# One encoder layer in float32 on one core: attention scores as full-array matmuls, shifted tiles, and VectorE work reordered around the router

## What is computed

```python
x = layer_norm(x, emb_ln_g, emb_ln_b)
z = x @ w_in + b_in
q, k, v, u_sg, v_sg, glu_a, glu_g = jnp.split(z, SPLIT_POINTS, axis=-1)
a = neighbourhood_attention(q, k, v, rpb) @ w_a_o      # 8 heads of 64, 4x16 queries see 4x32 keys
bb = (gelu(u_sg) * spatial(w_s, layer_norm(gelu(v_sg)))) @ w_b_o
c = silu(layer_norm(depthwise_conv(glu_a * sigmoid(glu_g)))) @ w_c_o
g = sigmoid(x @ w_gate + b_gate)                       # three gates of width 1024
m = (g0 * a + g1 * bb + g2 * c) @ w_o + b_o
x = layer_norm(ALPHA * x + m, ln1_g, ln1_b)
f = grouped_moe(x, w_router, b_router, w_e1, w_e3, w_e2)  # 16 experts, two for each token
x = layer_norm(ALPHA * x + f, ln2_g, ln2_b)
```

## Time and profile before

| what | value |
| --- | --- |
| median of 3 runs | 785.61 us (785.34 to 785.99) |
| the profiled execution: time, and span of its instructions | 787.25 us, 785.5 us |
| TensorE busy | 756.5 us (96%) |
| VectorE, ScalarE, GpSimd busy | 610.3, 428.2, 71.0 us |
| mean granted clock of TensorE | 0.988 of full speed |
| DMA | 175.53 MB, mean 223 GB/s |

### The profile page before, as it was taken

The page is one execution under the profiler, slowest core; times in us unless marked ns, Lnnn a source line. Parts: engine busy times, 40 slices in busy tenths (PEclk is TensorE's granted clock), DMA queues, the critical chain, the costliest instruction groups (busy, mean ns, idle before and its releaser), DMA issues.

```text
span 785.5 us, 10752 instructions
## 1 busy us (share of the span) xinstructions
PE 756.5 (96%) x3580; PEld 619.8 (79%) x3580; DVE 610.3 (78%) x827; ACT 428.2 (55%) x577; POOL 71.0 (9%) x94
## 2 busy tenths in 40 slices
PE   3999999999999999999999979999999999999995
PEld 3888878888888888888888857888888888888873
DVE  5699977675777875634547888999999999999977
ACT  5422134547432234623231365888888888888861
POOL 5000000000000000000011112111111111110314
PEclk9999999999999999999999988999999999999998
DMA  9844557132444343323279677999999999999882
GB/s 299 243 108 100 175 150 207 55 92 72 117 123 131 111 138 104 103 86 108 81 244 350 213 258 237 335 387 382 382 381 380 387 387 368 375 368 369 255 171 111
DMA packets 137490, 175.53 MB, mean 223 GB/s; under 512 B 15419, under 2 KB 75559, under 8 KB 137431
## 3 DMA queue, kind: packets, MB, share of 16 engines
q1 hardware_dynamic: 128896, 154.95, 58.7%
q0 software_dynamic: 7616, 19.34, 8.2%
q10 hardware_dynamic: 934, 0.69, 0.3%
HBM read 164.06 MB, written 19.11 MB: 233 GB/s over the span
## 4 chain that ended last, share of the span: by engine, by line
PE 92%; DVE 4%; ACT 2%; DMA 1%; issue 1%; POOL 0%; SPq 0%; DVEq 0%; ACTq 0%
PE bank L1834 27%; PE bank L1836 27%; PE bank L1835 27%; PE bank L2129 2%; PE bank L1870 1%; PE bank L2050 1%; DMA x_in<-in_x_sample_dram 1%; PE bank L1829 1%; PE bank L2144 1%; PE bank L2230 1%; PE bank L1880 1%; DVE w_lo L1053 1%; PE bank L2089 1%; PE bank L2220 0%; PE bank L2221 0%
## 5 line engine op out<-in xcount | busy, mean ns | idle before, releaser
L1053 DVE TENSOR_TENSOR w_lo<-raw,w_hi 128x1024 fp32r<-128x1024 f32 x103 | 125.1, 1221 | 80.4 <-ACT w_hi L721 80.1
L721 ACT CAST w_hi<-raw 128x1024 fp32r<-128x1024 f32 x103 | 107.1, 1048 | 105.3 <-PE bank L1836 100.7
L1834 PE MATMUL bank<-xT_hi,w_hi 128*128 128x512 f32 x352 | 139.9, 397 | 2.9 <-DVE xT_lo L1091 1.8
L1836 PE MATMUL bank<-xT_hi,w_lo 128*128 128x512 f32 x352 | 138.8, 394 | 0.0
L1835 PE MATMUL bank<-xT_lo,w_hi 128*128 128x512 f32 x352 | 137.8, 392 | 0.0
L1834 PEld LDWEIGHTS bank<-xT_hi,w_hi 128*128 128x128 f32 x352 | 66.5, 189 | 18.2 <-issue 3.4
L1834 PE MATMUL bank<-w_hi,xgT_hi 128*128 128x512 f32 x198 | 80.1, 404 | 0.8 <-issue 0.8
L1836 PEld LDWEIGHTS bank<-xT_hi,w_lo 128*128 128x128 f32 x352 | 66.4, 189 | 14.7
L1835 PEld LDWEIGHTS bank<-xT_lo,w_hi 128*128 128x128 f32 x352 | 66.6, 189 | 14.5
L1836 PE MATMUL bank<-w_hi,xgT_lo 128*128 128x512 f32 x198 | 77.5, 392 | 0.0
L1835 PE MATMUL bank<-w_lo,xgT_hi 128*128 128x512 f32 x198 | 77.3, 390 | 0.0
(11 more groups left out here) (288 smaller groups left out, 1532.6 us busy)
## 6 DMA issues: line engine op xcount, KB each, us to landing
raw_more<-in_w_e_dram SPq DMA_DIRECT2D x48, 512.0 KB
raw<-in_w_e_dram SPq DMA_DIRECT2D x48, 512.0 KB, 9.3
raw_late<-in_w_e_dram SPq DMA_DIRECT2D x48, 512.0 KB
raw_rows<-in_w_e_dram SPq DMA_DIRECT2D x48, 512.0 KB, 9.6
raw<-in_w_in_dram SPq DMA_DIRECT2D x28, 512.0 KB, 6.5
raw<-in_w_gate_dram SPq DMA_DIRECT2D x24, 512.0 KB, 3.8
y_scratch<-zeros SPq DMA_DIRECT2D x8, 512.0 KB, 5.0
raw<-in_w_o_dram SPq DMA_DIRECT2D x8, 512.0 KB, 3.7
```

The costliest lines, as they stand in the source:

```text
L721: act.copy(hi_slot(j), raw_slot(j)).then_inc(hi_cast, 1)
L1053: dve.tensor_tensor(lo_slot(j), raw_slot(j), hi_slot(j).bitcast(F32), ALU.subtract).then_inc(lo_cast, 1)
L1834: pe.matmul(out, hi_l, hi_r, start=start, stop=False)
L1836: return pe.matmul(out, lo_l, hi_r, start=False, stop=stop)
```

## The change

1. **Scores.** `q_pair` replaces `qT`. It holds, for two head pairs in turn, both sequences and four windows, a 128x128 block: head 0's queries on partitions 0 to 63 in columns 0 to 63, head 1's on partitions 64 to 127 in columns 64 to 127, and zeros elsewhere. One matmul over all 128 partitions then gives both heads' scores of a window: 4 for a group in place of 8. ScalarE writes the blocks with four instructions of 64 partitions in place of two of 128, and waits for the scores that read the buffer before. GpSimd writes the zeros once, after unit 2 and after the normalised input, which shares the memory, is stored.
2. **Where tiles lie.** Four 16-byte tiles become one of 64 bytes, `moments`, so everything behind them lies 64 bytes lower. `mT_hi` gets `LINE` and stays where it was. In the built program `xT_hi`, `xT_lo` and the first two branches now start on a multiple of 128 bytes; `q_pair`, `kT`, `v_win`, `vs`, `probs`, `probsT` and `w_sT` start 64 bytes past one; `mT`, the third branch and every operand of the experts' matmuls stay.
3. **VectorE around the router.** Eight constants move ahead of `add_mixed(0, t)`. `cast_lo(U_MOE)` moves from ahead of the router's ranks to behind `joint_lists(0, 0)`. `make_joint(2, 0)` and `make_joint(3, 1)` move behind `split_xg(0, 0)`.

```diff
-    rstd = sb(ctx, "rstd", [TT])
-    var_eps = sb(ctx, "var_eps", [TT])
-    minus_half = sb(ctx, "minus_half", [TT])
-    mu_rstd = sb(ctx, "mu_rstd", [TT])
+    moments = sb(ctx, "moments", [4, TT])
+    rstd, var_eps, minus_half, mu_rstd = [moments[:, k, :] for k in range(4)]
...
-    qT = sb(early, "qT", [WC, T])
+    q_pair = sb(early, "q_pair", [2, 2, 4, 2, GRID])
...
-    mT_hi = sb(late, "mT_hi", [DC, T], F32R)
+    mT_hi = sb(late, "mT_hi", [DC, T], F32R, LINE)
...
             act.wait_ge(*filled(("q", c)))
+            if c >= 2:
+                act.wait_ge(*filled(("scores", 2 * c - 3)))
             for s in range(2):
                 tokens = slice(s * SEQ, (s + 1) * SEQ)
-                o = act.activation(qT[:, c, tokens].rearrange("p (j r c) -> p r j c", j=4, r=ROWS),
-                                   bank(("q", c))[:, tokens].rearrange("p (r j c) -> p r j c", j=4, r=ROWS),
-                                   ACT.Identity, bias=column(V_IN + c))
+                for h2 in range(2):
+                    rows = slice(64 * h2, 64 * h2 + 64)
+                    o = act.activation(q_pair[rows, c % 2, s, :, h2, :].rearrange("p j (r c) -> p r j c", r=ROWS),
+                                       bank(("q", c))[rows, tokens].rearrange("p (r j c) -> p r j c", j=4, r=ROWS),
+                                       ACT.Identity, bias=column(V_IN + c)[rows, :])
...
+        pool.wait_ge(x0_stored, 16 * TT)
+        pool.wait_ge(unit_used, 3)
+        for h2 in range(2):
+            other = q_pair[64 * h2:64 * h2 + 64, :, :, :, 1 - h2, :].rearrange("p b s j q -> p (b s j) q")
+            pool.memset(other, 0.0).then_inc(q_blank, 1)
...
-            for h2 in range(2):
-                rows = slice(64 * h2, 64 * h2 + 64)
-                for j in range(4):
-                    o = pe.matmul(bank(("scores", g))[rows, j * P:(j + 1) * P],
-                                  qT[rows, hp, seq * SEQ + 64 * j:seq * SEQ + 64 * (j + 1)],
-                                  grid(kT[rows, hp, :], seq, WINDOW[j], KCOLS), start=True, stop=True)
+            if g == 0:
+                pe.wait_ge(q_blank, 2)
+            for j in range(4):
+                o = pe.matmul(bank(("scores", g))[:, j * P:(j + 1) * P],
+                              q_pair[:, hp % 2, seq, j].rearrange("p h q -> p (h q)"),
+                              grid(kT[:, hp, :], seq, WINDOW[j], KCOLS), start=True, stop=True)
```

17 lines of the change are left out of this document (9 added, 8 removed).

## The result

The changed kernel takes **781.39 us** (median of 6 runs, 779.67 to 784.03), beside 786.11 for the kernel before on the same chip (785.34 to 787.70, 6 runs). The ratio is 0.994, with a 95% interval from 0.992 to 0.996. The forecast was 776.7 with a range from 774.3 to 779.4. It had the sign right, but only half of the gain came, and the time lies outside of the range.

The account below looks back on a forecast made before the run. TensorE, busy for 96% of the span, was taken as the bound. Scores, less the stall at the first turn, gave 5.0 us and tile addresses 3.9: 8.9 off 785.6 makes 776.7 us, range 774.3 to 779.4.

Parts of the forecast that it names:

- Scores, 0.72 a group: Attention scores on TensorE: each group takes 1.11 us in place of 1.84, a gain of 0.72.
- D: Score matmuls: a padded pass costs as much as the two it replaces, so scores give nothing; 781.7 us, chance 0.05.
- E: Eight score groups: un-tiled passes lose side-by-side work, +1.5 us a group, +12 in all; 793.7 us, chance 0.03.
- The 1.1 us kept in the range for the float32 operands off the multiple: Attention's 160 float32 passes, moved off a 128-byte multiple: cost 0 to 1.1 us, taken as 0.
- Where tiles lie, 3.9: Units with `xT` or a branch as operand: start on a 128-byte multiple gives 5.44 us each, 3.9 us saved in all.
- Rival B: Tile addresses: start address isn't the cause, or matters only for the stationary side; 780.6 or 779.3 us, chance 0.08.
- The stall at the first turn, 0.45: First transposes of softmax probabilities: TensorE arrives before they are ready and loses 0.45 us.
- Attention product 6: TensorE's wait for VectorE's `branch_lo` grows from 0.75 to 1.6 us or more; group 7's whole 0.72 is lost.
- Rival A: More gained: no stall at turn 0 (0.45), full clock at the first gathered tokens (about 1); 775.2 us, chance 0.13.
- VectorE around the router, 0: Moved constants, subtraction of unit 72 and one-hot matrices around the router: no effect on time, bounds -1.2 to +0.4 us.
- The bound that I gave was +0.4: Reordered VectorE work around the router: upper bound of its cost, +0.4 us.
- Expert 0 starts as long after them as before: Router: the time from the ranks to the start of expert 0 stays unchanged.

Follow-up runs that it names:

- the padded run: 32 unused bytes a partition added between the statistics tile and the token tiles of the changed kernel; 786.95 us (one run).

## Why the prediction was wrong, point by point

**Scores, 0.72 a group.** Right: 0.23 + 0.89, units 20 to 23 with their scores went from 8.55 to 7.71 us each, 0.84, which is 0.72 for the scores, 0.1 for leaving the half-height form and 0.05 for the unit, less rounding. Rivals D and E are out. The 1.1 us kept in the range for the float32 operands off the multiple was not needed: 0.889 us on a multiple and off it. The rule in the Trainium skill, "TensorEngine Tiling (Array Packing)", sections "Overview" and "Tiling Modes", that small contractions are best packed, would have made this slower; the traces show the un-packed form 0.6 us shorter a group, 0.111 us a pass against 0.094 for four times the array.

**Where tiles lie, 3.9.** Right in every unit, and the padded run confirms the cause. Rival B is out. The page "SBUF — State Buffer" of the Trainium skill, section "Operand start alignment", asks for four bytes only; by the runs a float32r operand that keeps to this rule can still cost 3% of its matmuls.

**The stall at the first turn, 0.45.** This is the term that failed worst: **2.15 us measured, 1.7 missed.** The step that failed is "TensorE reaches the turn after two groups at 0.72 and one shorter unit (0.05), at 134.24." Exp 0 I had at 130.0 and it started at 128.98, which is the same once the 1.0 us is taken off by which this execution ran ahead from unit 2 on (the kernel before had half clock at 19.5 us, this one not). But TensorE was there at 131.54: the 134.24 forecast less this 1.0, and less the 1.7 us that the tile addresses give in the units ahead. The sum booked those in full under "Where tiles lie" and never set them against this wait, as if the softmax moved along with TensorE. I took ScalarE's queries and table load for what sets exp, and they do follow TensorE: the table was loaded at 127.70. But the earlier trace rows show 1.02 us of idle time ahead of exp, which ended with VectorE's maximum. VectorE's chain set exp, before and after, and I didn't follow it back: it ends at a weight transfer behind `v_win` in SyncE's queue. With half of `v_win` later 1.3 us came back, and the reordered division gave the rest.

**Attention product 6.** Right: the wait rose from 0.91 to 1.97, and group 7's gain was lost there.

**The clock.** Not in the sum. A pause of 2 us at full clock was followed by half clock in some executions, which cost 1.6 to 1.7 us. Rival A thought of the clock only as a gain at the router. In the profiled execution (781.51) it is the whole distance to the kernel's level (779.8); the median, 781.4, lies beside it.

**VectorE around the router, 0.** The ranks and the constants were right. The step that failed is the reload: "now it goes at 471.2, still ahead of the second of them, which waits for unit 73. Its buffer is for unit 96, a whole ring away. 0." It asked who waits for the reload, not what else is moved at that moment. It goes beside the one transfer on which TensorE waits, and the subtraction that releases it runs beside GpSimd's issue. The pair of profiles with and without the third part puts 0.56 us on this; over all profiles with the same half clock it is 0.2 to 0.7. The bound that I gave was +0.4. "Expert 0 starts as long after them as before" looks right in the profiles, 16.37 against 16.43 us behind the ranks; but the kernel before had 10.2 us of half clock there and the changed one 6.8. Profiles with 6.8 and the old order have 15.7 to 15.8.

**The experts.** 284.0 us between their first and last matmul before, 284.6 after; forecast unchanged. A pass through the loop takes 17.73 us in place of 17.69; the extra 0.04 lies in matmuls 0.232 apart in place of 0.227 behind the transposes of the gathered tokens. It stands in both profiles of the changed kernel and in those of six others, among them the ones with scores alone and with addresses alone; not in those of the kernel before, of the router order alone, of the changed kernel without it, or of the three with the cast of unit 72 elsewhere. Each of the first two parts alone has it and both together without the third do not, so it is not the sum of the parts. **This stays open**: no edit explains the grouping, and none was tried for it.

In sum: 8.9 less 1.7 at the turn, 0.6 at the gather and 0.6 in the experts is 6.0, beside 5.6 measured between the levels; the medians, which hold the clock's part too, differ by 4.7. The range was too narrow because it held bounds for single costs, but none for a chain that stands still while TensorE gets earlier.

## What to carry to other kernels

When TensorE gets faster by several us, don't only price the work: for each wait ahead, find the chain that ends it, follow it back to what does not move with TensorE (a transfer, a queue), and set the whole gain up to there against its slack. An idle bracket ahead of an instruction names who was late, which is the chain to follow. And ask of each moved instruction, and of each transfer that it releases, what it will run beside.

## What the hardware showed that I had not expected

- A float32r operand that starts 32 bytes past a multiple of 128 costs 7 ns per 512-column matmul in either role (5.60 in place of 5.44 us for 24); 64 bytes past it, 7 ns when stationary and 2 ns when moving.
- With a 512 KB load issued 0.7 us behind an indirect gather, and VectorE's subtraction under way at the issue, the gather's first packets land at 4.0 to 4.1 us in place of 2.1 or 2.9. GpSimd's own issue takes 1.57 in place of 1.16; this goes with the subtraction, since with a load alone beside them 25 of 28 such issues took 1.00 to 1.01.
- At the first turn and at product 6 TensorE's granted clock fell to half behind 3 of 14 pauses of 1.8 to 2.2 us, and behind none of 14 of 1.0 us or less; a stretch of 3.4 us at half clock cost 1.0 to 1.1 us in the first units and 1.6 to 1.7 behind product 6.
- One issue held SyncE's queue for 5.6 to 6.1 us in every profile, five issues behind the first `v_win` load, whether it was itself a `v_win` load of 256 KB or a weight load of 512 KB, while the DMA engines were busy for less than half (0.46 of 95.80 to 106.00 in the changed kernel).
